# An encoder trunk on one core: the fourth sum of each seven-product quad made by a DMA with addition, GpSimd drained before the last norm, and the last norm's gains multiplied later

## The reference

```python
for l in range(DEPTH):                     # DEPTH = 2
    h = rmsnorm(x, norm_mix[l])
    proj = h @ w_in[l]                     # attention and a short gated convolution
    ...
    x = x + jnp.concatenate([o_attn, o_conv], axis=-1) @ w_out[l]
    h = rmsnorm(x, norm_ffn[l])
    x = x + (jax.nn.silu(h @ w_gate[l]) * (h @ w_up[l])) @ w_down[l]
return rmsnorm(x, norm_final)              # x * rsqrt(mean(x*x) + eps) * gain
```

## Time and profile before

| | |
|---|---|
| median of 3 runs | 2184.8 us (2184.66 to 2184.8) |
| the profiled execution's own time | 2184.7 us |
| its span, first to last instruction | 2182.9 us |
| TensorE busy | 2167.3 us, 99% of the span |
| DVE busy | 1729.0 us, 79% |
| ACT busy | 1203.4 us, 55% |
| POOL busy | 209.6 us, 10% |
| HBM read | 441.31 MB, 203 GB/s over the span |

### The profile page before, as it was taken

How to read it: one execution, slowest core, us unless ns; L and a number is a source line. 1 busy time by engine, 2 the same in 40 slices (tenths; PEclk the granted TensorE clock), 3 DMA queues, 4 the chain that set the end, 5 groups by cost and what they waited for, 6 DMA issues and landing times.

```text
span 2182.9 us, 27605 instructions
## 1 busy us (share of the span) xinstructions
PE 2167.3 (99%) x10481; PEld 1808.6 (83%) x10481; DVE 1729.0 (79%) x2139; ACT 1203.4 (55%) x1646; POOL 209.6 (10%) x246
## 2 busy tenths in 40 slices
PE   9999999999999999999999999999999999999997
PEld 7888888888888888888888888888888888888886
DVE  6776676888889887788766676768988888888887
ACT  6445564555556555555544555555555555555554
POOL 0031120000000000000001212200000000000000
PEclk9999999999999999999999999999999999999999
DMA  9655455756765675667666544556577567657574
GB/s 348 208 175 173 170 174 174 230 184 209 243 219 188 234 231 196 196 227 226 223 203 209 173 156 173 186 184 199 190 246 236 189 208 243 204 190 239 189 237 157
DMA packets 131556, 449.42 MB, mean 206 GB/s; under 512 B 15072, under 2 KB 15712, under 8 KB 131040
## 3 DMA queue, kind: packets, MB, share of 16 engines
q1 hardware_dynamic: 115344, 416.40, 53.6%
q0 software_dynamic: 14784, 28.32, 7.6%
q10 hardware_dynamic: 1296, 2.94, 0.4%
HBM read 441.31 MB, written 2.10 MB: 203 GB/s over the span
## 4 chain that ended last, share of the span: by engine, by line
PE 96%; DVE 2%; ACT 1%; issue 0%; POOL 0%; DMA 0%; SPq 0%; ACTq 0%; DVEq 0%
PE bank L1674 18%; PE bank L1675 17%; PE bank L1676 17%; PE bank L1648 14%; PE bank L1651 7%; PE bank L1686 7%; PE bank L1687 7%; PE bank L1688 7%; PE bank L1839 1%; PE bank L1798 1%; PE bank L1821 1%; DVE wlo L1023 0%; DVE wlo L1016 0%; PE bank L1777 0%; POOL o_rms L560 0%
## 5 line engine op out<-in xcount | busy, mean ns | idle before, releaser
L626 ACT ACTIVATE whi<-raw 128x1024 fp32r<-128x1024 f32 x596 | 625.9, 1060 | 469.5 <-PE bank L1676 285.9
L1016 DVE TENSOR_TENSOR wlo<-raw,whi 128x1024 fp32r<-128x1024 f32 x596 | 724.6, 1232 | 179.4 <-ACT whi L626 166.2
L632 ACT ACTIVATE whi<-raw 128x1024 fp32r<-128x1024 f32 x368 | 343.2, 950 | 234.1 <-PE bank L1676 176.3
L1023 DVE TENSOR_TENSOR wlo<-raw,whi 128x1024 fp32r<-128x1024 f32 x368 | 390.5, 1088 | 77.0 <-ACT whi L632 75.9
L1648 PE MATMUL bank<-xg,whi 128*128 128x512 f32 x1280 | 406.9, 399 | 0.5 <-DVE wlo L1247 0.5
L1674 PE MATMUL bank<-whi,xg 128*128 128x512 f32 x1024 | 402.7, 393 | 0.0
L1676 PE MATMUL bank<-whi,xg 128*128 128x512 f32 x1024 | 399.1, 390 | 0.0
L1675 PE MATMUL bank<-wlo,xg 128*128 128x512 f32 x1024 | 398.9, 390 | 0.0
L1651 PEld LDWEIGHTS bank<-xg,wlo 128*128 128x128 f32 x1280 | 240.4, 188 | 56.9
L1651 PE MATMUL bank<-xg,wlo 128*128 128x256 f32 x1280 | 252.1, 278 | 0.0
L1676 PEld LDWEIGHTS bank<-whi,xg 128*128 128x128 f32 x1024 | 192.2, 188 | 40.2
(11 more groups left out here) (159 smaller groups left out, 2768.0 us busy)
## 6 DMA issues: line engine op xcount, KB each, us to landing
raw<-w_gu_dram SPq DMA_DIRECT2D x352, 512.0 KB, 5.1
raw<-w_in_dram SPq DMA_DIRECT2D x188, 512.0 KB, 4.4
raw<-w_down_dram SPq DMA_DIRECT2D x176, 512.0 KB, 5.2
raw<-w_out_dram SPq DMA_DIRECT2D x64, 512.0 KB, 4.4
raw<-w_gu_dram POOLq DMA_DIRECT2D x64, 256.0 KB, 6.1
raw<-w_down_dram POOLq DMA_DIRECT2D x28, 256.0 KB, 4.1
swapped<-qk POOLq DMA_DIRECT2D x32, 128.0 KB, 2.7
x_t<-x_t_dram SPq DMA_DIRECT2D x8, 256.0 KB, 6.4
```

The source lines that it names most:

```text
L626: act.activation(whi[:, blk.slot(k)], raw[:, slot, half * UNIT_KT:(half + 1) * UNIT_KT, :], ACT.Copy).then_inc(hi_ready, 1)
L632: act.activation(whi[:, quad.slot(n), 0:tiles.stop - tiles.start], raw[:, quad.raw(), tiles, :], ACT.Copy).then_inc(hi_ready, 1)
L1016: dve.tensor_tensor(wlo[:, blk.slot(k)], raw[:, slot, half * UNIT_KT:(half + 1) * UNIT_KT, :], lo_bits(whi[:, blk.slot(k)]), ALU.subtract) ...
L1023: dve.tensor_tensor(wlo[:, quad.slot(n), into], raw[:, quad.raw(), tiles, :], lo_bits(whi[:, quad.slot(n), into]), ALU.subtract).then_inc( ...
```

## The change

There are three edits. First, the sum of all four blocks is no longer made by DVE. `third_sum` goes, and POOL issues a second DMA with addition for each quad, `add_bha`, from tile 1 to tile 0 of the same place in SBUF; ACT waits for its landing (`bha_added`) before split 3. In the gu pairs with three quads POOL's order is given by `add_three`. Second, POOL has a drain of its own between the last of these DMAs and the two operations of the last norm. Third, the last norm's gains on chunks 0 and 1 are no longer multiplied between the last splits, but after the left block's residual.

```diff
+            def add_bha(quad):
+
+                pool.wait_ge(weights_ready, quad.split[0] + 1)
+                pool.wait_ge(first_sums, quad.number + 1)
+                pool.dma_start(raw[:, quad.raw(), 0, :], raw[:, quad.raw(), 1, :], accum_op=ALU.add
+                               ).then_inc(bha_added[quad.raw()], 16)
+
+            def add_three(quads):
+                add_b(quads[1])
+                add_bha(quads[0])
+                add_b(quads[2])
+                add_bha(quads[1])
+                add_bha(quads[2])
...
-                for k in range(1, GU_SEVENS):
-                    add_b(plan.pairs[layer, "gu", 0].quads[k])
-                for p in range(1, NGU // 2):
-                    for quad in plan.pairs[layer, "gu", p].quads.values():
+                add_three(plan.pairs[layer, "gu", 0].quads)
+                for p in range(1, NGU // 2 - 1):
+                    add_b(plan.pairs[layer, "gu", p].quads[0])
+                    add_three(plan.pairs[layer, "gu", p].quads)
+                for pair in (plan.pairs[layer, "gu", NGU // 2 - 1], *(plan.pairs[layer, "down", p] for p in range(2))):
+                    for quad in pair.quads.values():
                         add_b(quad)
-                for p in range(NCH // 2):
-                    for quad in plan.pairs[layer, "down", p].quads.values():
-                        add_b(quad)
+                        add_bha(quad)
+
+            pool.drain()
...
                 split_quad(quad, 2, slice(2, 4))
-                act.wait_ge(third_sums, quad.number + 1)
+                act.wait_ge(bha_added[quad.raw()], 16 * quad.added)
                 split_quad(quad, 3, slice(0, 2))
...
-            def third_sum(quad):
-
-                o, bha = (raw[:, quad.raw(), i, :] for i in (0, 1))
-                dve.wait_ge(first_sums, quad.number + 1)
-                dve.tensor_tensor(o, o, bha, ALU.add).then_inc(third_sums, 1)
...
                     split(left, 20, DUNITS)
-                    final_gains(0)
-                    split(right, 19, 20)
-                    final_gains(1)
-                    split(right, 20, DUNITS)
+                    split(right, 19, DUNITS)
                     add_residual(left, pair)
-                    final_gains(2)
+                    for c in range(NCH - 1):
+                        final_gains(c)
```

More of the change, by code:

```diff
@@ L383, in build_program @@
     b_added = [sem(f"b_added{i}") for i in range(NRAW)]
+    bha_added = [sem(f"bha_added{i}") for i in range(NRAW)]
     sum_copied = sem("sum_copied")
@@ L411, in build_program @@
     second_sums = sem("second_sums")
-    third_sums = sem("third_sums")
     form_step = sem("form_step")
@@ L1066, in turn @@
                 split(units[1][0], units[1][1], units[1][1] + 1)
-                third_sum(quad)
                 second_parts(quad)
@@ L1154, in gu_three @@
                 second_sum(q0)
-                third_sum(q0)
                 if prior is not None:
@@ L1165, in gu_three @@
                 first_sum(q2)
-                third_sum(q1)
                 split(right, 5, 6)
                 second_sum(q2)
-                third_sum(q2)
                 second_parts(q1)
```

## The result

| | before | after |
|---|---|---|
| median | 2184.7 us | 2196.3 us (2195.3 to 2196.6) |
| the profiled execution's own time | 2184.7 us | 2195.3 us |
| its span | 2182.9 us | 2193.4 us |

The ratio is 1.0053, with a 95% interval of 1.004 to 1.0065. The forecast was 2180.6 us, the range 2179.4 to 2184.0: wrong, and on the other side of no change. Three of the executions behind this document took far longer than the rest of their kernel (2389 us in run 7, 9061 us in run 8, 3649 us of the kernel before beside runs 9 to 11) and are counted nowhere.

A forecast was written before the change was run, and what follows sets the result against it. PE, busy 99% of the span, was taken as the bound. 2184.7 - 0.35 - 3.0 - 0.95 = 2180.4 us; the runs' median lies 0.1 above, so 2180.5, stated as 2180.6; range 2179.4 to 2184.0.

The forecast's parts named there:

- the second: Gu pairs and down turns: the new DMA additions land in time or within PE's slack; price 0.
- PE's slack of 2.9: Down turn: of 5.25 us between ACT's split 3 and PE, splits take 1.06 and 1.22, leaving 2.9.
- My 4.2 us: Assumed time from issue to landing of an addition within SBUF, with 2.7 and 8.9 us as ends.
- 6.1 us at q0 of the gu pairs: Allowed time from first sum to landing there, called the tight place; the down turn's room was 7.0 us.
- The rival of the late transfer: PE stalls at q0's third product in 20 gu pairs, 20 us per microsecond past 6.1; some 2238 us at 8.9; chance 0.17.
- The sign of being wrong: The prediction is wrong if additions within SBUF take over 6 us, or the last drain stays at microseconds.
- Step 1: Third sum leaves DVE: 0.35 us gained in the first gu pairs, between 0 and 1.2.
- Step 2, POOL's queue: 92 more issues of 0.865 us on POOL, 80 us; q2's addition delayed but hidden by 4 us.
- Step 3: Early POOL drain, 9.1 or 16 us, hidden before the last norm; short drain at the end gains 3.0 us.
- edit 3: The early POOL drain behind the last new DMA, forecast to gain 3.0 us at the program's end.
- Step 4: Last norm's gains moved: PE's last matmul 0.95 us earlier, between 0 and 1.0.
- edit 1: Removing DVE's third sum: 0.35 us in the first gu pairs, upper end 1.2.

The follow-up runs named there:

- run 7: Kernel after, but in the second down pair SyncE loads a turn's plain units before its quad: 2183.8 us, spread 2180.5 to 2187.3.
- run 8: Kernel before plus one more GpSimd drain between the last layer's gu and down stages: 2181.6 us, against 2184.6 beside it.
- runs 9 to 11: Early q1 addition with gu third sums by DMA, 2179.4 us; with all third sums on VectorE, 2180.3; idle second-down-pair additions cut to 8 KB, 2180.7.
- Run 3: Kernel after, but in the second down pairs VectorE makes the third sum and GpSimd issues equal-sized idle additions no turn waits for: 2180.9 us.
- run 4: Kernel after with VectorE's third sums and idle additions in the second down pairs, ScalarE waiting for each idle landing before split 3: 2198.9 us.
- Run 9: Kernel after, but down third sums on VectorE and the addition from HBM for q1 of each first gu pair issued ahead of the norm's power: 2179.4 us.
- run 2: Kernel before with only the early drain and the late gains, no addition within SBUF: 2180.7 us, ratio 0.9982.
- runs 5 and 6: Kernel after, in the second down pair: 1.5 MB loaded a quad turn in place of 2, 2180.4 us; or every second quad's third sum on VectorE, 2180.4 us.

## Why the prediction was wrong

**The step that failed** is the second, in these words: "in the down turn 0.2 after, of which PE's slack of 2.9 swallows all. Price: 0". Three things in it:

- *The slack was spent once for each turn.* It is there once. ACT's late split 3 frees the place late, so SP's loads for the turn after next go out late, and the next landing starts its count from there. In the kernel after the lateness came back with interest: the additions of quads 1 to 3 of layer 0 landed 3.7, 5.5 and 6.6 us after issue, and from quad 3 on PE paid every turn of that layer. I had written down the chain from landing to PE, and not the chain from split 3 back to the next landing. Runs 3 and 4, equal but for one wait and 18 us apart, show that the wait, and with it the way back to the next landing, is the cause.
- *Landing was taken as a duration.* My 4.2 us, and the ends 2.7 and 8.9, were times from issue. The quiet time was even shorter, 3.3. What mattered is an event: the last load issued before it, and 1.1 to 1.5 us more (so for 24 of the 25 additions of the kernel after with such a load still under way 2.2 us after their issue; the 25th came 2.5 after it, and why is open). From the kernel before this could be worked out: the last two loads of that turn were

```profile
L486 SPq DMA_DIRECT2D raw<-w_down_dram x2: 430/431/432, 1010.8 to 1011.3; - x2
DMA to landing us min/median/max: 5.3/5.7/6.1
```

  so the last landed at 1017.4, an addition behind it would at 1018.6, and ACT asked at 1017.84: 0.8 late, not 0.2. Run 3 shows it for quads 1 to 7 in a row; only the first addition of each layer was quick. The row that my 4.2 rested on was misread, too. The additions from HBM in the down stage do not have "few loads" beside them: in the second down pair of layer 0 all eight were issued with such loads under way for another 2.2 to 4.8 us, and landed 1.1 to 1.9 us after the last of these. The DMA engines moved 231 GB/s in that stretch:

```profile
DMA packets 7545, 25.44 MB, mean 231 GB/s; under 512 B 837, under 2 KB 837, under 8 KB 7540
```

- *Room was compared with room.* I took the smaller room for the tight place, 6.1 us at q0 of the gu pairs against 7.0 in the down turn. But in the gu pairs with three quads the loads ahead of q0's addition had at most 1.6 us still to go, and, as far as I read the order of these pairs, lateness isn't handed on there as in the row of down turns. The additions landed in time: no wait of PE for them in 64.

The rival of the late transfer had 0.17, named the gu pairs as its place and 20 us for each microsecond past 6.1 as its price. It named "the loads that SP has under way" as one possible reason, which is half of the mechanism, and argued against it that few are under way at q0's first sum, which is so for q0 and not for the down turns. It got the sign right, and place and price wrong: no addition in a gu pair held up PE. The sign of being wrong, additions over 6 us, came in the second down pairs only. The price is the loop's: 11.8 - 10.2 = 1.6 us a turn, from the point at which the 2.9 us are used up. In layer 0 the starts of PE's matmuls show gaps of 0.9, 1.8, 1.4, 1.5 and 1.9 us ahead of the third parts of quads 3 to 7, where 0.23 is usual: 6.4 of the 7.5 us. In layer 1 the lateness grows by 6.7: gaps of 0.8, 2.7 and 1.6 us ahead of the third parts of quads 4, 5 and 7, and between the last two a stretch at the lower clock, for which see below.

**Step 1** (0.35 us from the third sum) gave nothing: I let the addition for q1 land 4.1 us after issue, at 399.4; it took 4.4 and, behind the norm's power, was issued at 395.56. Run 9 shows that the 1.2 us of the upper end were there, behind this one landing, of which 0.4 came without the DMA's third sums, too.

**Step 2, POOL's queue**: as forecast. The issue cost 0.865 us (857 to 892 ns for the 92 new ones, beside a DVE 76% busy) and held up nobody. But POOL issued 0.54 us after the first sum's end, not 0.1.

**Step 3** (3.0 us for the drain): right; run 8 gives 3.0 alone, and the end is ACT's drain. In the kernel after, the drain of 10.7 us was hidden. Its length was within my 9 to 16 by luck: I had it from the count of DMAs, and run 8 shows that it doesn't follow the count. The last drain took 1.05 us, not well under 1, and was over before the last store. The Trainium skill ("VectorE: DVE Perf Modes", "The DRAIN you can't avoid") has about 12 ns for such a drain, by which edit 3 would be worth nothing and the time 3.0 us longer (the prediction has "lower", which is a slip); in none of these traces did POOL's come near that after a DMA.

**Step 4** (0.95 us for the gains): right. PE's wait of 0.86 is gone, the lateness falls from 14.6 us at the left block's last matmul to 13.5 at the right block's, and run 2 against run 8 gives 3.85 - 2.98 = 0.87.

**The range.** With edit 1 at its upper end the sum gives 2180.5 - 0.85 = 2179.65, not the 2179.4 of its lower bound. Nothing hung on it.

## What to carry to other kernels

This is one kernel's lesson, as a way to check. Before a wait on a DMA is put into a repeated turn, follow the chain all the way round: from the landing to the instruction that waits, to the buffer that it frees, to the loads issued into it, and back to the next landing. If that loop is longer than the turn, as here with 11.8 against 10.2 us, slack only delays the loss by a few turns; where it was shorter, or broken in every second turn (runs 5 and 6), the wait was free. And take a DMA's landing from what was issued before it, not from its size or a median.

## What the runs showed of the hardware

- An addition within SBUF of 256 KB landed 3.2 to 3.3 us after issue with little under way, one of 8 KB 2.0; behind loads of 512 KB both landed after the last of these, by 1.1 to 1.5 us and by 0.2 us.
- POOL's drain: 1.05 us with no DMA since the last one, 2.2 with 14, 8.5 to 9.4 with 110 to 188. With 216 it was 7.3 to 10.7, and ended 4.0 us after the last addition had landed in all six kernels.
- In the kernel after, layer 1, PE stood idle ahead of the third part of quad 5, which began at 2137.97. From 2139.18 to 2142.17 eight matmuls followed each other at 0.41 to 0.43 us in place of 0.227, at the lower level of the granted clock. A gap alone doesn't tell of it: after the gaps of layer 0, of 0.9 to 1.9 us, the matmuls kept their 0.227, and so they did after one of 2.9 us in run 4 and one of 3.8 us in run 7. Windows (us, busy and count of PE, PEld, DVE, ACT, POOL, then PE's clock, the DMA engines' share and GB/s):

```profile
2135.00:2139.00 4.00, 1.71 (x7) 1.12 (x7) 2.31 (x3) 3.40 (x4) 0.00 (x0) 0.97 0.08 12
2139.00:2142.00 3.00, 3.00 (x8) 2.32 (x8) 3.00 (x6) 1.13 (x2) 0.86 (x1) 0.50 0.92 310
```

  0.50 is 1.2 in place of 2.4 GHz. The eight took 3.4 us where they would have taken 1.8, so PE lost 1.6. That this came on top of the loop isn't shown: the additions of quads 5 to 7 landed 11.6 and 11.9 us apart, as in layer 0 (11.6 to 12.1), and PE did not wait at quad 6. The slow matmuls seem to have filled time that PE would have spent waiting.
